# Attention over four query tiles in a two-block f32 transformer kernel: the order of the tiles, the steps of the modulation sums, and the form of GpSimd's scaling

## Chip, cores and metric

One core of a Trainium2 chip. The metric is the device time of one execution in microseconds (us). The engines are named as in the profile: PE (TensorE matmuls; PEld is its weight load), DVE (VectorE), ACT (ScalarE), POOL (GpSimd), SP (SyncE, which here only issues DMAs).

## What is computed

Two blocks over 512 tokens of width 1024, all in f32. The first block has two layers: half a SwiGLU FFN, a token mixer, half a SwiGLU FFN. The second block (adaptive norms, a retention and a gated linear attention mixer, two more FFNs) is not touched here, except that nine modulation vectors that it needs are summed early, inside the first block's attention. The mixer of a layer, cut to what matters:

```python
q_nope, q_rope, k, v = ...                    # MLA, 4 heads; keys of 96
s = jnp.where(kpos <= qpos, q @ k.T * scale, NEG)       # causal, in blocks of 128 queries
o_mla = softmax(s) @ v_mla
a = softmax(s[:, 0]) - lam * softmax(s[:, 1])           # differential, 4 heads x 2 maps
o_diff = rms_norm(a @ v_diff, g) * (1 - lam_init)
p_c = softmax(where(valid, q @ k_cmp.T, NEG)) * valid   # NSA, 8 heads: 31 compressed keys
o_nsa = g0 * (p_c @ v_cmp) + g1 * o_slc + g2 * o_win    # selected and window keys; gates
y = concat(o_mla, o_diff, o_nsa) @ w_out
m = silu(c) @ ada_w + ada_b                             # 9 x 1024, for the second block
```

With 512 tokens every selected and window map is a plain causal map, so all 28 maps of a query tile have the same keys: those of its own tile and of all earlier ones.

## The kernel before

Every engine runs its own hand-written instruction stream, and semaphores order them. A layer is: FFN, norm, projections, attention, output projection, FFN. The weights of all dense products go through four slots of SBUF (`w_raw`, split into `w_hi` and `w_lo` by ACT line 884 and POOL line 840), and dense products are three fp32r matmuls per 128x128 block (line 2060).

**Attention** runs once per layer (layer 0 from 584.5 us, layer 1 from 1762.4 us). Its work is cut into units of two maps: 14 units per query tile (`UN`; two of MLA, four of differential heads, eight of NSA, `UNIT_MAPS`), four tiles, so 56 units (`NU`). The tiles are taken in the order 0, 1, 2, 3. Tile i has (i+1)*128 keys, so the units grow from 128 to 512 columns. All five engines step through t = 0 to 60 in the same pipeline, i, step = divmod(t, 14):

- PE: scores of unit t with their causal mask (lines 2317, 2319) into one of two pairs of PSUM banks, which is free once the exponentials of two score groups earlier have been read; the transposes of the probabilities of unit t-3 (line 2347; the second map's wait for DVE's copy of the unit before); the outputs of unit t-4 (line 2390, accumulated in banks 6 and 7).
- DVE: the row maximum of unit t (line 1714), the copy of the second transposed map of unit t-3 (line 1723), the reciprocal of unit t-1's sums (line 1728).
- ACT: the copy of the first transposed map of unit t-3 (line 1126), the exponentials of unit t with their sums (line 1135).
- POOL: the scaling of unit t's probabilities by the reciprocals (lines 848 to 856), in place. NSA maps are scaled by two columns at once (the reciprocal and the gate, line 852), the second differential maps too (reciprocal and lambda, line 854); the MLA maps and the first differential maps by one (line 856, no second operand).

Once per tile there is more. At step 1 (`AT_CMP`) PE makes the compressed scores (line 2326), and DVE subtracts their maxima; at step 2 ACT takes their exponential (line 1141) and DVE sums, inverts and gates them (`cmp_sums`, lines 1679 to 1686); at step 6 they are transposed. At steps 10 to 13 the differential heads are normalized: ACT loads the table of the root and then that of the exponential again (two table loads), DVE inverts. At step 4 of the next tile (`AT_LAST`), or after the last step for the last tile, the outputs of the bank 7 are split into `h_hi` and `h_lo`. The output projection starts when the last of these is written.

**Adaptive sums.** The nine modulation vectors (`ada_w`, 9216 columns) are summed in 18 steps per layer. One such step is 16 matmuls of 128x32 by 256 columns (line 2409) at the end of PE's step t, DVE's copy of the result (line 1769, the last thing DVE does in step t), four tiny matmuls at PE's step t+1, right after its scores and ahead of its transposes (line 2334), and DVE's addition (line 1733). Which t have one is a table (line 89):

```python
ADA_STEPS = [UN * i + at for i, steps in enumerate(((6, 8), (1, 5, 7, 9), (1, 3, 5, 7, 9), (1, 3, 5, 7, 9), (1, 3))) for at in steps]
```

so two in tile 0, four in tile 1, five each in tiles 2 and 3, and two after the last scores (t = 57 and 59). Their weights come in halves through a ring of three (SP, line 757): three halves ahead of the attention, then four slots of `w_out` (line 663), and only then the fourth half and those behind it.

## Time and profile before

| | |
|---|---|
| time, median of 3 runs | 3871.97 us (3863.09 to 3878.66) |
| the profiled execution | 3891.44 us, of which its span 3889.7 us |
| PE busy | 3633.1 us, 93% of the span |
| DVE, ACT, POOL busy | 1371.2, 1289.6, 1441.1 us (35%, 33%, 37%) |
| mean clock granted to TensorE | 0.954 of full speed |
| attention, layer 0 and layer 1 | 584.5 to 801.3 us and 1762.4 to 1967.0 us: 216.8 and 204.6 us |
| DMA | 83 GB/s on average |

The profile is one execution, seen by the hardware profiler. Busy time of an engine counts its instructions, overlaps taken once; matmul ends are modelled. The granted clock is a share of full speed: at 1.0 TensorE runs at 2.4 GHz, at 0.5 at 1.2 GHz; numbers between are averages over a stretch.

### The profile page before, as it was taken

Reading aid. Unit: us, or ns where it says so; the run is one execution under the profiler, and the core shown is the slowest. Engines: PE = TensorE matmul, PEld = TensorE weight load, DVE = VectorE, ACT = ScalarE, POOL = GpSimd, SP = SyncE. Lnnn points to the kernel's source line nnn. Section 1 sums busy time; section 2 is a strip of 40 time slices with the busy share of each in tenths; the row PEclk is TensorE's granted clock in tenths of the full one; section 3 lists DMA queues with packets and bytes.
Section 4 is the critical chain, followed back from the end, with each engine's and each line's share of the span. In section 5 each row is a group of like instructions: output and inputs, shape, how many; then the busy total and the mean of one; then the engine's idle time right before and its main releaser. Section 6 shows DMA issues by size and latency. Waiting matters only on the chain. (4 is left out here: it accounts for less than half of the span.)

```text
span 3889.7 us, 50750 instructions
## 1 busy us (share of the span) xinstructions
PE 3633.1 (93%) x18374; PEld 2863.5 (74%) x18374; DVE 1371.2 (35%) x1921; ACT 1289.6 (33%) x2011; POOL 1441.1 (37%) x756
## 2 busy tenths in 40 slices
PE   7999899999999999798999996999998998779998
PEld 6888575578887888565578884888886785547886
DVE  4223544542325232554642326111114303552112
ACT  4223334543224222334543224312123234234222
POOL 4444233434444444334434442222222340013443
PEclk8999897999999999898999998999998998979999
DMA  4333342323333332342323332222212322012331
GB/s 133 95 96 91 75 122 77 108 69 96 95 91 98 95 96 87 73 127 87 110 68 96 96 91 72 59 65 60 65 53 56 86 82 65 1 44 81 97 97 60
DMA packets 569027, 322.35 MB, mean 83 GB/s; under 512 B 30266, under 2 KB 563360, under 8 KB 568480
## 3 DMA queue, kind: packets, MB, share of 16 engines
q1 hardware_dynamic: 568864, 320.22, 28.3%
q8 instruction: 97, 1.59, 0.2%
q14 instruction: 66, 0.54, 0.0%
HBM read 318.08 MB, written 2.10 MB: 82 GB/s over the span
## 5 line engine op out<-in xcount | busy, mean ns | idle before, releaser
L840 POOL TENSOR_TENSOR w_lo<-w_raw,w_hi 128x1024 fp32r<-128x1024 f32 x516 | 1267.7, 2457 | 2187.7 <-ACT w_hi L884 2187.7
L884 ACT ACTIVATE w_hi<-w_raw 128x1024 fp32r<-128x1024 f32 x516 | 547.6, 1062 | 1876.6 <-PE psum L2060 1767.6
L2060 PE MATMUL psum<-h_hi,w_hi 128*128 128x512 f32 x1328 | 544.1, 410 | 45.4 <-DVE h_ctx_lo L1457 22.8
L2060 PE MATMUL psum<-xg_hi,w_hi 128*128 128x512 f32 x1408 | 553.0, 393 | 12.2 <-DVE xg_lo L1409 10.4
L2060 PE MATMUL psum<-xg_lo,w_hi 128*128 128x512 f32 x1408 | 549.7, 390 | 0.0
L2060 PE MATMUL psum<-xg_hi,w_lo 128*128 128x512 f32 x1408 | 549.5, 390 | 0.0
L2060 PE MATMUL psum<-h_lo,w_hi 128*128 128x512 f32 x1328 | 530.3, 399 | 0.0
L2060 PE MATMUL psum<-h_hi,w_lo 128*128 128x512 f32 x1328 | 528.4, 398 | 0.0
L2060 PE MATMUL psum<-a_hi,w_hi 128*128 128x512 f32 x1232 | 433.3, 375 | 5.0 <-DVE a_lo L1525 4.2
L2060 PE MATMUL psum<-a_lo,w_hi 128*128 128x512 f32 x1232 | 434.2, 376 | 0.0
L2060 PE MATMUL psum<-a_hi,w_lo 128*128 128x512 f32 x1232 | 432.5, 374 | 0.0
L2060 PEld LDWEIGHTS psum<-h_hi,w_hi 128*128 128x128 f32 x1328 | 253.9, 191 | 133.1 <-issue 38.1
L2060 PEld LDWEIGHTS psum<-xg_hi,w_hi 128*128 128x128 f32 x1408 | 265.5, 189 | 72.2 <-DVE xg_lo L1409 14.0
L2060 PEld LDWEIGHTS psum<-xg_lo,w_hi 128*128 128x128 f32 x1408 | 265.6, 189 | 56.1 <-issue 1.2
L2060 PEld LDWEIGHTS psum<-xg_hi,w_lo 128*128 128x128 f32 x1408 | 265.5, 189 | 55.2
L2060 PEld LDWEIGHTS psum<-h_hi,w_lo 128*128 128x128 f32 x1328 | 254.4, 192 | 59.1
L2060 PEld LDWEIGHTS psum<-h_lo,w_hi 128*128 128x128 f32 x1328 | 254.9, 192 | 56.8 <-issue 5.4
L2060 PEld LDWEIGHTS psum<-a_hi,w_hi 128*128 128x128 f32 x1232 | 218.6, 188 | 49.9 <-DVE a_lo L1525 5.9
L2060 PEld LDWEIGHTS psum<-a_hi,w_lo 128*128 128x128 f32 x1232 | 219.6, 188 | 43.0
L2060 PEld LDWEIGHTS psum<-a_lo,w_hi 128*128 128x128 f32 x1232 | 219.1, 188 | 41.2
L1484 DVE TENSOR_TENSOR gated<-silu_g,psum 128x512 f32<-128x512 f32 x66 | 37.6, 597 | 501.3 <-ACT silu_g L937 501.3
L1520 DVE TENSOR_TENSOR gated<-psum,rstd 128x512 f32<-128x512 f32 x88 | 60.9, 692 | 420.8 <-PE psum L2060 420.8
(409 smaller groups left out, 4387.8 us busy)
## 6 DMA issues: line engine op xcount, KB each, us to landing
w_raw<-ffn_w SPq DMA_DIRECT2D x120, 512.0 KB, 3.8
w_raw<-ffn_w_gate SPq DMA_DIRECT2D x88, 512.0 KB, 3.8
w_raw<-ffn_w_up SPq DMA_DIRECT2D x88, 512.0 KB, 3.8
ada_raw<-ada_w SPq DMA_DIRECT2D x72, 512.0 KB, 4.5
w_raw<-ffn_w_down SPq DMA_DIRECT2D x64, 512.0 KB, 4.1
w_raw<-w_in SPq DMA_DIRECT2D x60, 512.0 KB, 3.8
w_raw<-ffn_w_down SPq DMA_DIRECT2D x32, 384.0 KB, 3.4
w_raw<-w_out SPq DMA_DIRECT2D x24, 512.0 KB, 4.0
```

What stands on the lines that cost most here:

```text
L840: nc.gpsimd.tensor_tensor(w_lo[:, i, :], w_raw[:, i, :], w_hi[:, i, :].bitcast(F32), ALU.subtract).then_inc(lo_ready, 1)
L884: nc.scalar.activation(w_hi[:, pos, :], w_raw[:, pos, :], ACT.Copy).then_inc(hi_ready, 1)
L1484: last = nc.vector.tensor_tensor(gated[:, i, o:o + n], silu_g[:, i, o:o + n], up, ALU.mult)
L1520: nc.vector.tensor_tensor(gated_1[:, i, :], psum[:, 3 * i + 1, :], rstd[:, 0:T], ALU.mult).then_inc(scaled.sem, 1)
L2060: last = nc.tensor.matmul(dst, w[:, pos, k * P:(k + 1) * P], rhs[g][r](k0 + k), start=k == 0 and m == 0, stop=k == nk - 1 and m == 2)
```

## The change

It does three things. The tiles are taken in the order 3, 2, 1, 0 (`TILE_AT`), so the units shrink from 512 to 128 columns; every use of the tile number that stands for tokens (queries, keys, gates, masks, places in `h_hi` and `h_lo`) goes through `TILE_AT`, while the counts of the semaphores go on by the order in time. The adaptive sums have the steps 0, 2, 5, 7, 9 of the first tile in time, 1, 3, 5, 7, 9 of the second and the third, 1, 5, 8 of the fourth, and none after the last scores. POOL's scaling of the MLA and first differential maps has a second column, `ones`. Outputs at a tile's first unit also wait for the adaptive sums in the first tile.

```diff
+TILE_AT = tuple(range(TT))[::-1]
-ADA_STEPS = [UN * i + at for i, steps in enumerate(((6, 8), (1, 5, 7, 9), (1, 3, 5, 7, 9), (1, 3, 5, 7, 9), (1, 3))) for at in steps]
+ADA_STEPS = [UN * i + at for i, steps in enumerate(((0, 2, 5, 7, 9), (1, 3, 5, 7, 9), (1, 3, 5, 7, 9), (1, 5, 8))) for at in steps]
...
             def attention(layer):
                 for u in range(NU):
-                    n = (u // UN + 1) * P
+                    tile = TILE_AT[u // UN]
+                    n = (tile + 1) * P
...
                         else:
-                            last = nc.gpsimd.tensor_scalar(rows, rows, inv, None, ALU.mult)
+                            last = nc.gpsimd.tensor_scalar(rows, rows, inv, ones[:, 0:1], ALU.mult, ALU.mult)
...
                         dve.wait_ge(*scores_done(layer, SCORE_AT["unit", t] + 1))
-                        nc.vector.tensor_reduce(neg_max[:, 2 * t:2 * t + 2], psum[:, b:b + 2, 0:(i + 1) * P], AX_X, ALU.max,
+                        nc.vector.tensor_reduce(neg_max[:, 2 * t:2 * t + 2], psum[:, b:b + 2, 0:(TILE_AT[i] + 1) * P], AX_X, ALU.max,
...
-                            for b in range(u // UN + 1):
+                            for b in range(TILE_AT[u // UN] + 1):
                                 last = nc.tensor.transpose(psum[:, 4 + m, b * P:(b + 1) * P], probs[:, u % 3, m, b * P:(b + 1) * P], ident[:])
...
-                        if at == 0 and j:
-
-                            pe.wait_ge(*diff_std(layer, 2 * j))
+                        if at == 0:
+                            if j:
+
+                                pe.wait_ge(*diff_std(layer, 2 * j))
                             pe.wait_ge(*ada_read(layer, 2 * sum(n <= t for n in ADA_STEPS)))
```

How the streams move, at the three places that the prediction speaks of. Rows of the change have its own line numbers, which are 1 to 5 higher.

PE at the start of the attention, before (steps 0 to 2; `ISA` and `REGISTER_ALU` are waits and counters):

```order
L2317 MATMUL psum<-k_mla,q_mla 128x128 x2
L2319 MATMUL psum<-causal_b,ident_b 128x128 x2
L2317 MATMUL psum<-k_mla,q_mla 128x128 x2
L2319 MATMUL psum<-causal_b,ident_b 128x128 x2
L2322 REGISTER_ALU
L2326 MATMUL psum<-k_cmp,q_nsa 128x31 x8
L2312 REGISTER_ALU
L2317 MATMUL psum<-k_diff,q_diff 128x128 x2
L2319 MATMUL psum<-causal_b,ident_b 128x128 x2
```

and now (steps 0 to 2, up to the first scores of step 2):

```order
L2321 MATMUL psum<-k_mla,q_mla 128x512 x2
L2323 MATMUL psum<-causal_b,ident_b 128x128 x2
L2412 REGISTER_ALU
L2414 MATMUL psum<-ada_raw,cond 32x256 x8
L2321 MATMUL psum<-k_mla,q_mla 128x512 x2
L2323 MATMUL psum<-causal_b,ident_b 128x128 x2
L2326 REGISTER_ALU
L2330 MATMUL psum<-k_cmp,q_nsa 128x31 x8
L2335 ISA
L2338 MATMUL psum<-cond_sum,mod_rows 128x2 x2
L2315 REGISTER_ALU
L2321 MATMUL psum<-k_diff,q_diff 128x512 x2
```

The left-out parts of the diff replace the tile's number by `TILE_AT` in the same way. The scores have 512 columns where they had 128, and an adaptive sum stands behind the first scores, its small matmuls behind the compressed scores, and another sum follows behind the scores of step 2.

DVE at steps 2 and 3 of the first tile, before:

```order
L1714 TENSOR_REDUCE neg_max<-psum 128x2
L1726 REGISTER_ALU
L1728 RECIPROCAL scaled_inv<-exp_sum 128x2
L1679 TENSOR_REDUCE cmp_stats<-cmp_p 128x8
L1680 REGISTER_ALU
L1681 RECIPROCAL cmp_stats<-cmp_stats 128x8
L1682 REGISTER_ALU
L1683 TENSOR_TENSOR cmp_stats<-cmp_stats,gates 128x8
L1685 REGISTER_ALU
L1686 TENSOR_SCALAR cmp_stats<-cmp_stats,cmp_any 128x8
L1713 REGISTER_ALU
L1714 TENSOR_REDUCE neg_max<-psum 128x2
```

and now:

```order
L1731 RECIPROCAL scaled_inv<-exp_sum 128x2
L1682 TENSOR_REDUCE cmp_stats<-cmp_p 128x8
L1683 REGISTER_ALU
L1684 RECIPROCAL cmp_stats<-cmp_stats 128x8
L1685 REGISTER_ALU
L1686 TENSOR_TENSOR cmp_stats<-cmp_stats,gates 128x8
L1688 REGISTER_ALU
L1689 TENSOR_SCALAR cmp_stats<-cmp_stats 128x8
L1769 REGISTER_ALU
L1772 COPY mod_rows<-psum 128x256
L1716 REGISTER_ALU
L1717 TENSOR_REDUCE neg_max<-psum 128x2
```

DVE's copy of the adaptive sum (`mod_rows`) of step 2 stands behind the whole of `cmp_sums`; before, no adaptive sum was at a step 2.

PE at the end of the attention, before:

```order
L2383 MATMUL psum<-cmp_pt,v_cmp 64x128 x2
L2390 MATMUL psum<-probs_t_134,v_slc 64x128 x8
L2390 MATMUL psum<-probs_t_132,v_win 64x128 x8
L2402 REGISTER_ALU
L2409 MATMUL psum<-ada_raw,cond 32x256 x8
L2331 REGISTER_ALU
L2334 MATMUL psum<-cond_sum,mod_rows 128x2 x2
L2414 REGISTER_ALU
L2415 REGISTER_ALU
L2418 ISA
L2060 MATMUL psum<-h_hi,w_hi 128x512
```

and now:

```order
L2351 MATMUL psum<-ident,probs 128x128 x2
L2395 MATMUL psum<-probs_t_132,v_win 64x128 x2
L2342 REGISTER_ALU
L2351 MATMUL psum<-ident,probs 128x128 x2
L2388 MATMUL psum<-cmp_pt,v_cmp 64x128 x2
L2395 MATMUL psum<-probs_t_134,v_slc 64x128 x2
L2395 MATMUL psum<-probs_t_132,v_win 64x128 x2
L2419 REGISTER_ALU
L2423 ISA
L2063 MATMUL psum<-h_hi,w_hi 128x512
```

The last transposes and outputs stand as x2 where they stood as x8 (one and four blocks of keys, for two maps or two heads), and the adaptive sum with its small matmuls is gone from between the last outputs and the output projection (line 2060, now 2063).

## Rows read from the trace of the kernel before

**Rows 1.** The page, share of the 40 slices: clock granted to TensorE, in tenths.
```profile
PEclk8999897999999999898999998999998998979999
```

**Rows 2.** Stretches: us, then PE, PEld, DVE, ACT, POOL busy (count), PEclk, DMA, GB/s.
```profile
584.50:624.40 39.90, 35.74 (x232) 21.66 (x232) 16.69 (x56) 18.54 (x76) 15.57 (x28) 0.60 0.21 69
624.40:673.30 48.90, 46.00 (x359) 28.18 (x356) 24.33 (x67) 23.22 (x78) 18.75 (x29) 0.77 0.27 87
673.30:729.80 56.50, 52.60 (x459) 32.36 (x458) 30.34 (x68) 27.65 (x78) 23.30 (x29) 0.88 0.30 94
729.80:786.00 56.20, 51.87 (x514) 33.22 (x512) 33.94 (x65) 30.09 (x72) 26.48 (x27) 1.00 0.31 95
786.00:801.30 15.30, 11.64 (x132) 9.03 (x132) 5.94 (x13) 4.03 (x9) 3.05 (x4) 0.89 0.11 36
1762.40:1800.50 38.10, 32.72 (x232) 19.89 (x232) 16.16 (x55) 18.28 (x76) 15.35 (x28) 0.69 0.22 72
1800.50:1842.60 42.10, 38.73 (x350) 23.84 (x348) 23.63 (x65) 23.17 (x80) 18.64 (x30) 0.91 0.33 101
1842.60:1893.80 51.20, 48.13 (x470) 30.64 (x466) 30.06 (x68) 28.04 (x80) 23.51 (x30) 0.97 0.33 104
1893.80:1949.40 55.60, 52.11 (x518) 33.27 (x514) 33.35 (x64) 30.22 (x73) 26.58 (x28) 1.00 0.31 96
1949.40:1967.00 17.60, 13.09 (x133) 10.20 (x133) 6.77 (x14) 4.03 (x9) 3.05 (x4) 0.81 0.11 31
```

**Rows 3.** The same columns, 10 us inside the first tile, layer 0.
```profile
600.00:610.00 10.00, 10.00 (x68) 5.98 (x60) 3.15 (x11) 2.33 (x12) 1.77 (x4) 0.50 0.52 167
```

**Rows 4.** Waits of PE in layer 0's attention: us in total, times, longest.
```profile
PE psum L2347 <- DVE probs_t L1723: 8.0, 5, 2.8
```

**Rows 5.** Groups by line on POOL: busy, mean ns, idle before.
```profile
L852 POOL TENSOR_SCALAR probs<-probs,scaled_inv,gates 128x128 f32<-128x128 f32 (+3 forms) x128 | 77.0, 612 | 156.4 <-DVE scaled_inv L1728 156.4
L856 POOL TENSOR_SCALAR probs<-probs,scaled_inv 128x128 f32<-128x128 f32 (+3 forms) x64 | 68.9, 1088 | 53.0 <-DVE scaled_inv L1728 53.0
```

**Rows 6.** Who waited for POOL's line 856: us, times.
```profile
  PEld psum L2347: 0.3, 1
```

**Rows 7.** Timeline of the first steps: start, us, engine, what [idle before].
```profile
586.70 1.08 PE L2326 MATMUL psum<-k_cmp,q_nsa 64*128 64x31 f32 x16 [0.74 <-ACT probs L1135]
...
590.44 0.80 PE L2317 MATMUL psum<-k_diff,q_diff 32*128 32x128 f32 x4 [1.02 <-ACT probs L1135]
```

**Rows 8.** Timeline of the 512-key tile, layer 0.
```profile
729.76 1.98 PE L2317 MATMUL psum<-k_mla,q_mla 96*128 96x512 f32 x4
...
740.24 0.40 ACT L1141 ACTIVATE cmp_p<-cmp_p 128x248 f32<-128x248 f32 x1
740.67 0.41 DVE L1679 TENSOR_REDUCE cmp_stats<-cmp_p 128x8 f32<-128x248 f32 x1 [1.22 <-ACT cmp_p L1141]
...
741.87 1.23 DVE L1714 TENSOR_REDUCE neg_max<-psum 128x2 f32<-128x1024 f32 x1
...
742.62 1.07 PE L2409 MATMUL psum<-ada_raw,cond 128*32 128x256 f32 x16
...
743.62 1.13 PE L2317 MATMUL psum<-k_diff,q_diff 32*128 32x512 f32 x4
...
743.76 0.42 DVE L1769 COPY mod_rows<-psum 128x256 f32<-128x256 f32 x1
...
744.38 0.20 ACT L1135 ACTIVATION_READ_ACCUMULATOR probs<-psum,neg_max 128x1 f32 x1
```

**Rows 9.** Timeline of SP's queue before and at layer 0's attention.
```profile
563.18 1.80 SPq L757 DMA_DIRECT2D ada_raw<-ada_w  x3
570.88 17.24 SPq L663 DMA_DIRECT2D w_raw<-w_out  x4
```

**Rows 10.** Timeline of the end of layer 0's attention.
```profile
785.52 1.23 DVE L1714 TENSOR_REDUCE neg_max<-psum 128x2 f32<-128x1024 f32 x1
...
801.33 0.49 PE L2060 MATMUL psum<-h_hi,w_hi 128*128 128x512 f32 x1 [1.19 <-DVE h_lo L1702]
```

More of the change, by code:

```diff
@@ L851, in attention @@
                             at = 3 * h + (1 if kind == "slc" else 2)
-                            last = nc.gpsimd.tensor_scalar(rows, rows, inv, gates[:, u // UN, at:at + 1], ALU.mult, ALU.mult)
+                            last = nc.gpsimd.tensor_scalar(rows, rows, inv, gates[:, tile, at:at + 1], ALU.mult, ALU.mult)
                         elif second:
@@ L1124, in attention @@
                             act.wait_ge(*o_done(layer, u - 1))
-                        n = (u // UN + 1) * P
+                        n = (TILE_AT[u // UN] + 1) * P
                         nc.scalar.activation(probs_t[u % 2][:, 0, 0:n], psum[:, 4, 0:n], ACT.Copy).then_inc(probs_t_act.sem, 1)
@@ L1129, in attention @@
                         act.wait_ge(*max_ready(layer, t + 1))
-                        n = (i + 1) * P
+                        tile = TILE_AT[i]
+                        n = (tile + 1) * P
                         for m in range(2):
@@ L1137, in attention @@
                         last.then_inc(exp_ready.sem, 1)
-                        at = slice(i * P, (i + 1) * P)
+                        at = slice(tile * P, (tile + 1) * P)
                         if step == AT_CMP_EXP:
@@ L1699, in last_low @@
                 def last_low(i):
-                    at = slice(i * P, (i + 1) * P)
+                    at = slice(TILE_AT[i] * P, (TILE_AT[i] + 1) * P)
                     dve.wait_ge(*o_hi_ready(layer, 3 * i + 3))
@@ L1721, in attention @@
                             dve.wait_ge(*o_done(layer, u - 1))
-                        n = (u // UN + 1) * P
+                        n = (TILE_AT[u // UN] + 1) * P
                         nc.vector.tensor_copy(probs_t[u % 2][:, 1, 0:n], psum[:, 5, 0:n]).then_inc(probs_t_dve.sem, 1)
@@ L1735, in attention @@
                     if t < NU:
-                        at = slice(i * P, (i + 1) * P)
+                        at = slice(TILE_AT[i] * P, (TILE_AT[i] + 1) * P)
                         if step == AT_CMP_TURN:
@@ L2312, in attention @@
                             pe.wait_ge(*scores_read(layer, v - 2))
-                        n = (i + 1) * P
+                        tile = TILE_AT[i]
+                        n = (tile + 1) * P
                         banks = [psum[:, score_banks(("unit", t)) + m, :] for m in range(2)]
@@ L2316, in attention @@
                             q, k, _ = key_values(*head)
-                            nc.tensor.matmul(banks[m][:, 0:n], q(slice(i * P, (i + 1) * P)), k(n), start=True, stop=False)
+                            nc.tensor.matmul(banks[m][:, 0:n], q(slice(tile * P, (tile + 1) * P)), k(n), start=True, stop=False)
                         for m in range(2):
@@ L2326, in attention @@
                                     last = nc.tensor.matmul(psum[:, score_banks(("cmp", i)) + g, c * CMP_BLOCK:c * CMP_BLOCK + NC],
-                                                            q_nsa[rows, c, i * P:(i + 1) * P], k_cmp[rows, :], start=True, stop=True)
+                                                            q_nsa[rows, c, tile * P:(tile + 1) * P], k_cmp[rows, :], start=True, stop=True)
                             last.then_inc(scores_done.sem, 1)
@@ L2383, in attention @@
                                 nc.tensor.matmul(o_place(kind, h), v_cmp[:, g, c * DV:(c + 1) * DV], cmp_pt[:, g, :], start=True, stop=False)
-                        for b in range(j + 1):
+                        for b in range(TILE_AT[j] + 1):
                             for x, head in enumerate(UNIT_MAPS[at]):
@@ L2390, in attention @@
                                 last = nc.tensor.matmul(o_place(kind, h), v(b), probs_t[u % 2][:, x, b * P:(b + 1) * P],
-                                                        start=first and b == 0, stop=final and b == j)
+                                                        start=first and b == 0, stop=final and b == TILE_AT[j])
                         last.then_inc(o_done.sem, 1)
```

8 lines of the change are left out of this document (4 added, 4 removed).

## The prediction

> **What bounds the kernel now.** I read the page first. PE is busy for 93% of the span, and no other engine for more than 37%, so a change in the attention counts only by what it does to PE: its work, its idle time, and its clock. The granted clock over the span [rows 1] is 7 tenths in the slice in which layer 0's attention begins (the seventh, from 583 us) and 8 in that of layer 1 (the nineteenth, from 1750 us).
>
> Next come the stretches of the two attentions [rows 2]: of layer 0 the four tiles in the order of time (128, 256, 384, 512 keys) and the end behind the last scores, then the same of layer 1. Three things can be taken from them.
> - Idle time of PE: length less busy time, 4.2 + 2.9 + 3.9 + 4.3 + 3.7 = 19.0 us in layer 0, 5.4 + 3.4 + 3.1 + 3.5 + 4.5 = 19.8 us in layer 1.
> - Time at half clock: the clock has two levels, 1.0 (2.4 GHz) and 0.5 (1.2 GHz), so a mean of 0.60 over 39.9 us is 2 x 0.40 x 39.9 = 31.9 us at 1.2 GHz. The five stretches give 31.9, 22.5, 13.6, 0 and 3.4, together 71.4 us in layer 0; and 23.6, 7.6, 3.1, 0 and 6.7, together 41.0 us in layer 1.
> - PE's work, if it all ran at 2.4 GHz: busy time less half of the time at 1.2 GHz, 197.9 - 35.7 = 162.2 us and 184.8 - 20.5 = 164.3 us. That the two layers agree to 2 us says that the split into work, idle time and clock holds: the 12 us by which layer 0's attention is longer are clock.
>
> So an attention is about 163 us of work, 19.4 us of idle time and 20 to 36 us that half clock costs. The 512-key tile had no half clock in either layer, the 128-key tile had it for most of its length. Ten microseconds inside that tile [rows 3] have PE busy for 10.00 of 10.00 us at a clock of 0.50: a PE that never rests is not enough to get 2.4 GHz back while its matmuls are those of the short tile (few columns, keys of 32 to 96 rows).
>
> What PE waits for in an attention is mostly one thing, DVE's copy of the second map at the ends of tiles: 8.0 us in 5 waits, the longest 2.8 us at the end of the last tile [rows 4]. There the two table loads on ACT and the inversion on DVE stand between a maximum and the copy behind it.
>
> **Part 1, POOL's second column.** The widths are the same mix in both groups [rows 5]: 612 ns with two columns, 1088 ns with one. 64 x (1088 - 612) is 30.5 us less on POOL, 15 per layer. PE waited for line 856 once, 0.3 us [rows 6], because the transposes come three steps later. Between 0.3 and 30.5 us I take the 0.3 us that is in a row: nothing. What hides it is the lag of three steps, some 12 us of PE's own work in a long tile against 3.1 us of POOL.
>
> **Part 2, the order of the tiles: work.** The same matmuls are issued, so 163 us stay. The pieces that move are the last three transposes and four outputs of 512 keys, which leave the end of the attention and go into the steps of the next tile.
>
> **Part 3, idle time at the start.** With 512 keys the pipeline fills more slowly. In us from the first scores, with the durations of [rows 7, 8]: scores 1.98 and mask 0.3, to 2.3; adaptive sum 1.1, to 3.4; second scores to 5.7. Compressed scores 1.1 and the four small matmuls 0.6 fill to 7.4, but the third scores wait for the second pair of exponentials, which ends 2.7 us after the maximum begins (741.87 to 744.58), at 8.4: 1.0 us idle. Third scores 1.3, adaptive sum 1.1, fourth scores 1.3, to 12.1. Now PE's next instruction is the small matmul of the adaptive sum of step 2, and it needs `mod_rows`, which DVE copies only behind `cmp_sums`. That chain starts at 9.7: maximum and exponentials 2.7, compressed exponential 0.4, `cmp_sums` 1.2 (740.67 to 741.87), copy 0.4, and about 0.5 for five handovers: 14.9. So 2.8 us more idle, and the first transposes are queued behind that wait. Together 3.8 us, where the timeline of before has gaps of 0.74 and 1.02 us [rows 7]: +2 us per layer. The sum at step 0 has its weights (issued by 565 us); the fourth half is issued only behind the fourth `w_out` slot, at 588.1 us [rows 9], and might cost up to 2 us, within the same wait.
>
> **Part 4, idle time at the end.** From the last maximum to the output projection it is 15.8 us now [rows 10], 11.6 of 15.3 us of it busy [rows 2]. With 128 keys the chain is short, some 6 us by the differences of the shapes, but the 9 to 10 us saved are mostly PE work that is done earlier instead. The idle part falls from 3.7 to about 3 us. The stall of 2.8 us ahead of it stays, since it is DVE's and ACT's, and has less PE work beside it. I take -1 us per layer for the end (between -3.7, all of it, and +2).
>
> Idle time in all: +1 us per layer, +2.
>
> **Part 5, the clock.** This is the term that decides. By place, time at 1.2 GHz per layer:
> - Start: the fill has more and longer idle gaps than the one that ended at half clock in both layers, so I expect the clock to fall there again, in spite of the sum at step 0. But it then meets 512-key steps, and the nearest rows of long tiles, 13.6 and 3.1 us in the 384-key tile, say that it comes back sooner than in the short one. I take 12 us; bounds 0 and 31.9.
> - The borders: 512 to 384 keys 0, as 384 to 512 now. 384 to 256: 4 us, between 0 and 13.6.
> - The 128-key tile, entered over a border that cost the clock in both layers when it was passed the other way: 32 us, from 23.6 (layer 1's first stretch) to 45 (31.9 plus 3.3 for one more sum at half clock and 10 for the steps that still turn 256 keys).
> - The end: 4 us, from 3.4 to 6.7. It can reach into the output projection.
>
> Together 52 us, at a cost of half, 26 us per layer and 52 for both, against 35.7 + 20.5 = 56.2 us now: -4 us. **Sum:** -4 + 2 + 0 = -2 us. The sum is made against the profiled execution (3891.4 us), which becomes 3889; the median of the runs is 19.5 us lower, and the same difference there gives 3870 us. The spread of the three runs alone is 15.6 us.
>
> The row says that a fully busy PE stayed at 1.2 GHz for 10 us and more. The Trainium skill (TensorE: Matmul & The Clock Gate, What's actually happening) has a rule that speaks otherwise: "activity releases the throttle". Taken as busy time it would have the short tile back at full clock soon after each gap; the trace does not bear this out, and by it the result would be that of rival A.
>
> **Rival A, the clock holds** (22%). The adaptive sums at steps 0 and 2 keep PE occupied through the fill, the long tiles run on at 2.4 GHz, and in the short tile the clock comes in high and stays for most of it. For it: the 512-key tiles had no half clock at all, though they have stalls of 1 us and more. Against it: [rows 3], and the 2.8 us wait of part 3. Time at half clock falls to some 15 us per layer, the cost from 56 to 15 us: -41 + 2 = -39, 3833 us. It counts as faster from 45 us less of half clock over both layers on.
>
> **Rival B, the clock falls at the start and stays** (14%). This is the one on the other side. The wait for `mod_rows` behind `cmp_sums` lets the clock fall when the most expensive steps begin, and it takes the whole of the first ten steps to come back, 40 us. Less 4 us idle this costs 18 us per layer where the forecast has 6: +24, 3894 us. It decides from about 33 us at half clock at the start of each layer. For it: 24 and 32 us in the first stretch now. Against it: those were short matmuls.
>
> **Rival C, POOL was on the path** (3%): up to 30 us faster, 3842 us. Only the 0.3 us speak for it.
>
> **Forecast: no change that can be measured** (61%), 3870 us. A measurement of this kernel can tell about 0.5%, 19 us, from no change. Faster: A and C, less the part of A that stays within 19 us, with some of the forecast's own tail, 0.24. Slower: B and a little of the forecast's tail, 0.14. Same 0.62. The forecast alone holds 3850 to 3891. To leave out no more than 2 in 10 the range goes down to 3836, near A, and up to 3894, to B.
>
> **What the profile would show.** POOL's group of line 856 at about 612 ns (and 30 us less in all), and no change from it. PE busy from the first scores with a gap of about 1 us ahead of the third and one of 2 to 3 us ahead of the first transposes, ended by DVE's `mod_rows`. From the last maximum to the output projection 6 us instead of 15.8. Half clock near the start for about 12 us, none in most of the 512- and 384-key tiles, and most of the 128-key tile at 0.5. I am wrong if the first tile shows 1.0 throughout and the last one over 0.8 (A), or if the first tile's mean clock is under 0.7 (B), or if PE's idle time per attention leaves 17 to 23 us.

## The result and the profile after

| | before | changed |
|---|---|---|
| median, five runs each, one session | 3868.17 us (3863.01 to 3878.66) | 3887.01 us (3886.33 to 3888.64) |
| ratio to before, 95% interval | | 1.0040 (1.0021 to 1.0059) |
| profiled execution, its span | 3891.44, 3889.7 us | 3887.43, 3885.7 us |

The changed kernel is slower by 0.40%, where the forecast was 3870 us and no change that can be measured. (The ratios are not quotients of the medians; the two medians here are 18.8 us apart, 0.49%.) One execution of before in the second session took 8161 us and is left out of the ratios. 0.40% is within the 0.5% that the prediction called the same, and 3887 us within its range of 3836 to 3894, but the interval lies wholly above 1. The two profiled executions say something else: there the changed kernel is 4 us shorter, and the forecast had 2 us. The experiments had to explain that contradiction first.

These are the ten stretches that answer to [rows 2], of the changed kernel. The tiles of each layer stand in the order of time, now 512, 384, 256 and 128 keys, then the end behind the last scores; columns as in [rows 2].

```profile
583.50:644.70 61.20, 58.29 (x467) 34.83 (x468) 30.95 (x58) 29.17 (x70) 21.11 (x26) 0.86 0.31 97
644.70:696.90 52.20, 48.28 (x498) 32.06 (x497) 30.56 (x67) 27.86 (x78) 19.46 (x29) 1.00 0.33 102
696.90:740.90 44.00, 40.34 (x413) 26.80 (x412) 24.63 (x67) 23.03 (x78) 16.23 (x29) 0.96 0.40 121
740.90:783.80 42.90, 39.02 (x278) 24.56 (x278) 19.26 (x63) 17.71 (x77) 12.71 (x28) 0.64 0.12 38
783.80:795.00 11.20, 6.05 (x41) 3.52 (x39) 4.82 (x11) 5.77 (x15) 2.29 (x6) 0.73 0.00 0
1757.80:1818.90 61.10, 58.19 (x466) 34.85 (x467) 30.89 (x58) 29.20 (x70) 21.11 (x26) 0.86 0.31 97
1818.90:1871.20 52.30, 48.38 (x498) 32.13 (x497) 30.64 (x67) 27.89 (x78) 19.47 (x29) 1.00 0.33 102
1871.20:1915.20 44.00, 40.35 (x413) 26.85 (x412) 24.60 (x67) 23.03 (x78) 16.23 (x29) 0.96 0.40 121
1915.20:1958.00 42.80, 38.92 (x278) 24.57 (x275) 19.26 (x63) 17.63 (x76) 12.66 (x28) 0.64 0.13 38
1958.00:1969.20 11.20, 6.05 (x42) 3.53 (x39) 4.82 (x11) 5.82 (x15) 2.33 (x6) 0.73 0.00 0
```

The two layers now take 211.5 and 211.4 us. The split of the prediction, for layer 0: busy 58.29 + 48.28 + 40.34 + 39.02 + 6.05 = 192.0 us, so 19.5 us idle. Half clock is twice (1 - mean clock) times the length: 17.1 + 0 + 3.5 + 30.9 + 6.0 = 57.5 us, 57.1 before rounding. Work is 192.0 - 28.6 = 163.4 us. Work and idle time are those of before; the clock is what differs.

Ten microseconds in the changed kernel's last tile, the row that answers to [rows 3]:

```profile
755.00:765.00 10.00, 10.00 (x65) 6.25 (x68) 4.44 (x17) 5.06 (x22) 3.90 (x9) 0.50 0.22 76
```

PE rests for not a moment and stays at half clock, as in the short tile before. The two scaling groups on POOL, against [rows 5] (by line; busy, mean ns):

```profile
L854 POOL TENSOR_SCALAR probs<-probs,scaled_inv,gates 128x512 f32<-128x512 f32 (+3 forms) x128 | 76.5, 607 | 144.6 <-DVE scaled_inv L1731 144.6
L858 POOL TENSOR_SCALAR probs<-probs,scaled_inv,ones 128x512 f32<-128x512 f32 (+3 forms) x64 | 38.7, 615 | 86.8 <-DVE scaled_inv L1731 86.8
```

The second column brings 1088 ns down to 615 ns, 30.2 us less on POOL, as forecast. Nobody gains by it in the waits: POOL itself sits idle for 86.8 us ahead of these 64 instructions, waiting for DVE, and no instruction is listed as waiting for them, where before had one wait of 0.3 us.

### The profile page after: what moved, and what is told of

Its sections match the earlier page's. It is cut to its first block and busy times, and to the rows that moved or that the text cites. A ratio compares the mean times of both kernels' runs of the same rounds, so it can differ in the third digit from the quotient of the medians.

```text
span 3885.7 us, 50748 instructions
## 1 busy us (share of the span) xinstructions
PE 3628.5 (93%) x18374; PEld 2863.3 (74%) x18374; DVE 1369.1 (35%) x1921; ACT 1288.0 (33%) x2011; POOL 1411.5 (36%) x756
## 5 line engine op out<-in xcount | busy, mean ns | idle before, releaser
L2063 PE MATMUL psum<-xg_hi,w_hi 128*128 128x512 f32 x1408 | 552.6, 392 | 12.0 <-DVE xg_lo L1412 10.3
```

What stands on the lines that cost most here:

```text
L2063: last = nc.tensor.matmul(dst, w[:, pos, k * P:(k + 1) * P], rhs[g][r](k0 + k), start=k == 0 and m == 0, stop=k == nk - 1 and m == 2)
```

## The experiments

### Session one: a second profile of before, and the three parts alone

`before_again` is the kernel before without an edit. `two_columns` is the kernel before with the one line

```diff
-    last = nc.gpsimd.tensor_scalar(rows, rows, inv, None, ALU.mult)
+    last = nc.gpsimd.tensor_scalar(rows, rows, inv, ones[:, 0:1], ALU.mult, ALU.mult)
```

`order_only` has `TILE_AT` reversed, with the old table of sums and one column; `sums_only` has the tiles in the old order, the new table and one column:

```diff
-ADA_STEPS = ... (((6, 8), (1, 5, 7, 9), (1, 3, 5, 7, 9), (1, 3, 5, 7, 9), (1, 3))) ...
+ADA_STEPS = ... (((0, 2, 5, 7, 9), (1, 3, 5, 7, 9), (1, 3, 5, 7, 9), (1, 5, 8))) ...
```

> The unchanged kernel once more, to get a second profile of it. The first one was 19.5 us longer than the median of its runs (3891.4 against 3872.0), and the prediction carried the difference over to the changed kernel unchanged. Theory 1, the place is the clock in the attentions: this profile's span is near 3866 us and shows some 40 us less half clock in the two attentions than the 112.7 us of the first (20 us at 2 us of half clock for 1 us of time), with work near 163 us and idle time near 19 us per attention. Theory 2, the place is elsewhere (dense stretches, start, DMA): the attentions are 216.8 and 204.6 us long again, and the 20 us are missing outside them. If the profile comes out at 3890 again, profiling itself adds the difference, and the changed kernel's profile (3887.4 us, equal to its runs) would speak against that.

> Part 1 alone: the kernel before with the second column of ones on POOL. Theory 1 (prediction): POOL's group of line 856 falls from 1088 to about 612 ns, 30 us less on POOL, and the time stays within 3 us of before, since PE waited 0.3 us for it. Rival (C of the prediction): POOL was on the path of the fill, up to 15 us faster per layer. A third way: with DVE and POOL moved against each other the clock's stretches shift, and the time moves by 5 to 15 us either way with no change in PE's idle time.

> Part 2 alone: the tiles from the longest to the shortest, with the table of adaptive sums and the one column of before. Theory 1, the order costs the time, because the short tile now runs whole at half clock (30.7 us of it in the changed kernel) and its units' stalls lie behind it: 3885 to 3895 us, the short tile at 0.5 as before, and two more adaptive sums behind the last scores, each about 2 us with its waits. Theory 2, the sums at steps 0 and 2 cost the time (the wait for mod_rows behind cmp_sums): without them 3 us of idle time per layer go, the first stretch of half clock is shorter than 17 us, and the time is 3870 us or less.

> The new table of the adaptive sums alone, with the tiles in the order of before (128 keys first). Theory 1: in the fill of the short tile five sums instead of two add about 5 us of dense work to a tile of 37 us; the clock falls in the fill all the same, since a PE that was fully busy stayed at half clock there, so the first stretch stays between 20 and 35 us, and the time is within 10 us of before. Rival: the sums from the first step hold the clock through the fill and the short tile; the first stretches (30.7 and 23.9 us in the first profile) go, and the time is 10 to 20 us shorter than before.

Twelve timed runs of each against 35 of before (median 3874.72 us). "Half clock" in this table and the later ones is us per attention at 1.2 GHz in the profiled execution, layer 0 / layer 1, summed as above but before rounding.

| | median us | ratio (95%) | attention us | half clock us |
|---|---|---|---|---|
| before_again | 3872.20 | 0.9998 (0.9979 to 1.0017) | 203.0 / 203.0 | 37.5 / 37.5 |
| two_columns | 3877.80 | 1.0014 (0.9998 to 1.0030) | 209.3 / 203.1 | 51.2 / 37.5 |
| order_only | 3873.20 | 0.9991 (0.9973 to 1.0009) | 201.5 / 212.1 | 30.7 / 54.6 |
| sums_only | 3874.37 | 1.0003 (0.9985 to 1.0022) | 204.7 / 198.4 | 37.5 / 23.9 |

The first row resolves the contradiction. The stretches of layer 0 in the second profile of the unchanged kernel (128, 256, 384, 512 keys, end; columns as above):

```profile
584.00:618.30 34.30, 31.40 (x221) 19.13 (x222) 13.31 (x50) 15.69 (x68) 14.60 (x26) 0.65 0.26 80
618.30:660.90 42.60, 38.62 (x350) 23.73 (x349) 24.09 (x66) 23.79 (x81) 18.44 (x29) 0.92 0.32 100
660.90:712.30 51.40, 47.59 (x454) 29.97 (x453) 30.42 (x69) 28.11 (x79) 22.99 (x29) 0.97 0.32 104
712.30:767.60 55.30, 51.21 (x507) 32.56 (x505) 33.48 (x66) 28.78 (x75) 27.24 (x29) 1.00 0.30 96
767.60:787.00 19.40, 14.35 (x164) 11.19 (x162) 8.61 (x15) 7.22 (x13) 3.48 (x5) 0.91 0.09 28
```

Half clock 24.0 + 6.8 + 3.1 + 0 + 3.5 = 37.4 us, busy 183.2, idle 19.8, work 164.5 us. In [rows 2] the same program had 71.4 us in this place, with work of 162.2 and idle time of 19.0 us: a difference of 34 us at half clock. The split prices that at 17 us of time; the attention's length shows 13.8 us (216.8 to 203.0), because work and idle time come out 2.3 and 0.8 us apart the other way. Against this profile the changed one is 17.3 us longer in its span (3885.7 - 3868.4), and its attentions are 16.9 us longer (422.9 - 406.0). So between these two profiles the slowdown lies wholly inside the attentions: half clock 75.0 to 114.3 us costs 19.7, work and idle time give back 2.8, together 16.9 us.

None of the three parts alone is measurably slower; together their ratios would make 1.0008. Each profile again splits into work of 164 to 166 us, 19 to 21 us idle, and half of the time at 1.2 GHz. What moves is where the clock falls, and two identical layers of one execution can differ (30.7 and 54.6 us in order_only).

The second profile is not the typical one either. Every timed run has its mean granted clock on record, and twice (1 - clock) times its length is its time at half clock, for the whole program. Over the 139 timed executions of before in the four sessions that is 328 us on average, with clocks from 0.952 to 0.961. The first profile has 355 us and the second 300, the one about as far above the mean as the other is below it. The time outside the attentions is not constant either: 3468.3 us in the first profile and 3462.4 in the second, and between 3452 and 3474 us in all 18 profiles.

### Session two: the sum at step 2, and filling the short tile

`after_again` is the changed kernel unedited. `sum_at_3` moves one sum by one step:

```diff
-... (((0, 2, 5, 7, 9), (1, 3, 5, 7, 9), (1, 3, 5, 7, 9), (1, 5, 8))) ...
+... (((0, 3, 5, 7, 9), (1, 3, 5, 7, 9), (1, 3, 5, 7, 9), (1, 5, 8))) ...
```

`before_fill` is the kernel before with six matmuls added ahead of the scores of each of the first 17 steps; they write to columns 384 to 511 of the score banks, which nothing reads there. `after_fill` has the same six in the changed kernel's last 14 steps (`if t >= NU - UN`).

```diff
+                        if t < UN + 3:
+                            for _ in range(3):
+                                for m in range(2):
+                                    nc.tensor.matmul(banks[m][:, 3 * P:4 * P], ident_b[:], causal_b[:], start=True, stop=True)
```

> The changed kernel once more, beside the runs of before on the same chip. Split of the attention so far (work at full clock, idle time, half clock, all per attention): the kernel before in its second profile 164.4, 19.9, 37.5 us, the changed one 163.4, 19.5, 57.1 us, so all of the 8.4 us per attention by which it is longer is clock. Theory 1: the short tile at the end always runs at half clock; the profile again has 30.7 us there and some 57 us per attention, and the median is 10 to 20 us above before. Rival: how the stretches of half clock fall differs from session to session (before had 71.7 and 41.0 us in one profile, 37.5 and 37.5 us in another); then this profile has another number, the runs spread over 20 us as those of before do, and the difference to before is under 10 us.

> The changed kernel with the first tile's second adaptive sum at step 3 instead of step 2, so that its small matmuls no longer wait for mod_rows behind cmp_sums. Theory 1 (part 3 of the prediction): PE's idle time per attention falls by 2 to 3 us and the gap ahead of the first transposes by as much; and if that gap is what brings the clock down at the start, the first stretch of 17 us is gone or is 10 us as in the kernel with the order alone: 4 to 10 us faster per layer. Rival: the first fall comes from the fill as such; the stretch stays at 17 us, and only the idle time goes, 2 us per layer.

> The kernel before with six more matmuls per step (128x128 by 128 columns, bf16, the identity by the mask, into PSUM columns that nothing reads) ahead of the scores, in the 14 steps of the 128-key tile and the first three of the next. They compute nothing that is used. Each takes some 0.055 us at full clock, so 17 steps cost 5.6 us of PE work per attention. Theory 1, what keeps the short tile at half clock is how little its matmuls give the array to do (a PE busy for 10.00 of 10.00 us stayed at 0.50): the 23.9 us stretch in the first tile goes or is under 10 us, and the attention is 3 to 8 us shorter than 203 us in spite of the work. Rival, the clock follows the gaps in the fill alone: the first stretch stays near 24 us, the added matmuls cost double there, and the attention is 6 to 10 us longer.

> The changed kernel with the same six matmuls per step in the 14 steps of its last tile, the one with 128 keys, 4.6 us of work per attention. Theory 1: the 30.7 us at half clock in that tile go for the most part, the tile falls from 42.9 to some 32 us, and the kernel gains 10 to 20 us over both layers, to about the time of before or below it. Rival: the fall comes at the border from 256 to 128 keys and holds whatever follows: the tile stays at half clock and is 8 us longer per layer.

| | median us | ratio (95%) | attention us | half clock us |
|---|---|---|---|---|
| after_again | 3880.49 | 1.0019 (1.0002 to 1.0036) | 211.4 / 202.4 | 57.2 / 33.5 |
| sum_at_3 | 3868.14 | 0.9977 (0.9958 to 0.9996) | 201.7 / 198.8 | 30.5 / 23.4 |
| before_fill | 3858.08 | 0.9953 (0.9935 to 0.9971) | 195.8 / 195.8 | 3.4 / 3.4 |
| after_fill | 3873.32 | 1.0000 (0.9985 to 1.0015) | 204.6 / 202.4 | 30.1 / 23.4 |

**The changed kernel again.** 12 runs go from 3867.34 to 3891.33 us, where the first five lay within 2.3 us. Layer 1 had no fall in its last tile (3.4 us instead of 30.7), and its attention is 9.0 us shorter. All intervals for this kernel lie above 1, here and in session three, but nearer to 0.2% than to the 0.40% of the first five runs, and in both later sessions the lower end is 1.0002. The plain medians are 3.3 and 6.3 us above before (0.09% and 0.16%).

**The sum at step 2.** These two kernels were timed side by side and their intervals do not overlap. What PE did in the changed kernel from its second mask on (timeline: start, us, what, idle before):

```profile
588.29 0.28 PE L2323 MATMUL psum<-causal_b,ident_b 128*128 128x128 bf16 x2
588.49 1.08 PE L2330 MATMUL psum<-k_cmp,q_nsa 64*128 64x31 f32 x16
589.50 0.61 PE L2338 MATMUL psum<-cond_sum,mod_rows 128*128 128x2 f32 x4
591.36 2.08 PE L2321 MATMUL psum<-k_diff,q_diff 32*128 32x512 f32 x4 [1.25 <-ACT probs L1138]
593.37 0.39 PE L2323 MATMUL psum<-causal_b,ident_b 128*128 128x128 bf16 x2
593.69 1.94 PE L2414 MATMUL psum<-ada_raw,cond 128*32 128x256 f32 x16
595.56 2.08 PE L2321 MATMUL psum<-k_diff,q_diff 32*128 32x512 f32 x4
597.57 0.39 PE L2323 MATMUL psum<-causal_b,ident_b 128*128 128x128 bf16 x2
598.37 1.01 PE L2338 MATMUL psum<-cond_sum,mod_rows 128*128 128x2 f32 x4 [0.41 <-DVE mod_rows L1772]
599.24 1.95 PE L2351 MATMUL psum<-ident,probs 128*128 128x128 f32 x8
```

and in sum_at_3:

```profile
589.05 0.61 PE L2338 MATMUL psum<-cond_sum,mod_rows 128*128 128x2 f32 x4
590.91 2.08 PE L2321 MATMUL psum<-k_diff,q_diff 32*128 32x512 f32 x4 [1.25 <-ACT probs L1138]
592.92 0.39 PE L2323 MATMUL psum<-causal_b,ident_b 128*128 128x128 bf16 x2
593.24 2.08 PE L2321 MATMUL psum<-k_diff,q_diff 32*128 32x512 f32 x4
595.25 0.39 PE L2323 MATMUL psum<-causal_b,ident_b 128*128 128x128 bf16 x2
595.43 1.90 PE L2351 MATMUL psum<-ident,probs 128*128 128x128 f32 x8
597.27 1.07 PE L2414 MATMUL psum<-ada_raw,cond 128*32 128x256 f32 x16
598.27 1.13 PE L2321 MATMUL psum<-k_diff,q_diff 32*128 32x512 f32 x4
```

Both stop for the same 1.25 us ahead of the third scores, and both are at half clock behind it: scores of this shape take 2.08 us. In sum_at_3 the clock is back at 597.3 us (a sum in 1.07 us, scores in 1.13); in the changed kernel a sum takes 1.94 us, and full speed comes only at about 608. The first tile thus has 6.8 us of half clock instead of 17.1, in both layers. So the clock falls at the stall for the third scores in both, and the sum at step 2 puts off the return by 10 us. The edit moves the sum together with its small matmuls, so it does not show whether the 16 matmuls or the wait for `mod_rows` do this. That wait is only 0.41 us long here: at half clock PE is busy while DVE catches up.

The first tile is the smaller part of what this edit gains, though. In layer 0 of the two profiles, half clock falls from 57.1 to 30.5 us: 10.3 us less in the first tile, 6.8 more in the 256-key tile, and 23.9 less in the last tile, whose steps the edit does not touch. That tile in the two layers of sum_at_3, where the changed kernel has a clock of 0.64 twice (columns as in [rows 2]):

```profile
739.50:773.50 34.00, 29.13 (x278) 18.96 (x275) 18.86 (x63) 17.41 (x76) 12.63 (x28) 0.90 0.15 48
1898.80:1933.80 35.00, 30.24 (x279) 19.57 (x277) 18.84 (x63) 17.47 (x76) 12.71 (x28) 0.85 0.15 47
```

How one sum in the first tile changes the clock of the last, 150 us later, no run shows.

I had expected less idle time from this edit. It has more, 21.0 and 21.6 us against 19.5. The gain is clock only; that a faster PE reaches the same waits earlier is my reading, not tested.

**The fill.** In before_fill the short tile holds full clock throughout. Its first three stretches of layer 0:

```profile
584.10:614.30 30.20, 27.72 (x308) 19.01 (x306) 13.58 (x51) 16.30 (x70) 14.69 (x26) 1.00 0.30 89
614.30:654.40 40.10, 36.22 (x361) 22.81 (x360) 23.41 (x66) 23.08 (x79) 18.54 (x29) 1.00 0.34 106
654.40:705.10 50.70, 46.06 (x453) 29.03 (x452) 30.39 (x69) 28.19 (x79) 23.09 (x29) 1.00 0.33 105
```

The added matmuls of the first tile (groups by line and form: busy, mean ns, idle before):

```profile
L2318 PE MATMUL psum<-causal_b,ident_b 128*128 128x128 bf16 x89 | 7.5, 220 | 0.4 <-ACT probs L1135 0.4
```

Against before_again the attention has 34.1 us less at half clock, which is worth 17.0 us, for 9.5 us of added work (173.9 against 164.4) and 0.3 us more idle: 7.2 us, which is what its length shows (203.0 to 195.8). I had put the added work at 5.6 us; it cost 9.5. The whole profiled execution is 24.1 us shorter than that of before_again, of which the two attentions have 14.4; the other 9.7 us lie where the edit does nothing, so one profile against one other overstates it. The timed runs say 0.47%, 18 us. PE was busy for less of the time at the higher clock; over the same 10 us:

```profile
600.00:610.00 10.00, 9.38 (x108) 6.01 (x105) 4.21 (x17) 5.30 (x25) 4.42 (x10) 1.00 0.57 180
```

In after_fill the last tile holds the clock in both layers (3.4 us at half clock in each). In layer 0 that is worth 13.6 us, of which the added work takes 7.3 (170.7 against 163.4 us); the first tile's 17.1 and 13.7 us stay.

### Session three: how little filling is enough

`fill_thin` is before_fill with matmuls that load and drive 32 columns of the array instead of 128 (`banks[m][0:32, ...]`, `ident_b[:, 0:32]`). `fill_two` has two of the matmuls a step, `range(1)` for `range(3)`. `sums_fill` is sums_only with its first sums at 0, 3, 5, 7, 9 and two matmuls a step. `after_third` is the changed kernel again.

> The kernel before with six more matmuls per step in the same 17 steps as in the run before_fill, with the same 128 columns each and so nearly the same time on PE, but with 32 columns of the array in use instead of 128 (output on 32 partitions). They compute nothing that is used. In before_fill the half clock of an attention fell from 37.5 to 3.4 us and the attention from 203.0 to 195.8 us. Theory 1, it is how much of the array works that holds the clock: with a quarter of it the short tile falls to half clock again, 15 us or more per attention, and the attention is 202 us or longer. Theory 2, it is that PE has something to do at all (the gaps filled): the half clock stays at 3 to 10 us and the attention near 195 us.

> As before_fill, with two more matmuls per step instead of six, 17 steps (nothing that is used is computed). The six cost 9.5 us of work per attention (173.9 against 164.4 us). If two hold the clock as well, the attention is near 195.8 - 6 = 190 us, and the kernel some 10 us faster than before_fill. If two are too few, 10 to 24 us of half clock come back in the first tile, and it is between before_fill and before.

> The tiles in the order of before (128 keys first), the new table of sums with the first tile's second sum at step 3 instead of 2 (0, 3, 5, 7, 9), no sums behind the last scores, two more matmuls per step in the first 17 steps (nothing that is used is computed), one column on POOL. If dense work in the short tile holds the clock, the five sums and the two matmuls do it together: half clock under 10 us per attention, the end 15.7 instead of 19.4 us as with the sums alone, attention 190 us or less. If not, it has 24 to 37 us of half clock as with the sums alone (198.4 and 204.7 us).

> The changed kernel a third time, to settle how far it is from before: so far 1.0040 (1.0021 to 1.0059) and 1.0019 (1.0002 to 1.0036). Its profiles had the last tile at 42.8 us with 30.7 us of half clock three times and at 32.4 us with 3.4 us once. If the last tile takes the one or the other by chance, the runs spread over 20 us again (3867 to 3891 us last time) and the ratio is between 1.000 and 1.005. If the first session was the rule, they lie together near 3887 us.

| | median us | ratio (95%) | attention us | half clock us |
|---|---|---|---|---|
| fill_thin | 3866.29 | 0.9970 (0.9954 to 0.9985) | 199.2 / 199.1 | 13.7 / 13.7 |
| fill_two | 3868.40 | 0.9973 (0.9953 to 0.9993) | 199.5 / 199.4 | 23.9 / 23.9 |
| sums_fill | 3869.47 | 0.9978 (0.9959 to 0.9997) | 204.5 / 204.6 | 37.5 / 37.5 |
| after_third | 3881.99 | 1.0020 (1.0002 to 1.0038) | 211.4 / 205.2 | 57.2 / 39.8 |

The two short tiles of fill_thin, layer 0:

```profile
584.60:614.70 30.10, 28.05 (x306) 19.26 (x306) 13.72 (x51) 16.32 (x70) 14.60 (x26) 1.00 0.29 89
614.70:654.50 39.80, 36.22 (x361) 22.82 (x360) 23.22 (x66) 22.90 (x79) 18.45 (x29) 1.00 0.36 107
```

A quarter of the array's columns was enough for the short tile: its clock was 1.00 with 32 columns as with 128. This went against the theory that the share of the array decides. Yet the 384-key tile, which has no added matmul in either kernel, had 10.2 us at half clock where before_fill had none. Two matmuls a step still halve the fall in the short tile (13.7 us against 23.9). sums_fill was a miss: more sums and a filler in the short tile, and 20.5 us at half clock in it all the same, where sums_only had 10.2. That I cannot explain from these rows. Nor does its profile explain its ratio: the attentions are 3 us longer than those of before_again (409.1 against 406.0 us), while the timed runs are 0.22% faster than before, with an interval below 1.

### Session four: the column once more, the sum at step 3 once more, and combinations

`after_one_col` is the changed kernel with POOL's old form for the 64 maps. `sum_at_3_b` is sum_at_3 unedited. `sum3_fill` adds the thin matmuls of fill_thin in its last 14 steps. `fill_no_tail` is before_fill with no sums after the last scores:

```diff
-... (((6, 8), (1, 5, 7, 9), (1, 3, 5, 7, 9), (1, 3, 5, 7, 9), (1, 3))) ...
+... (((4, 6, 8), (1, 3, 5, 7, 9), (1, 3, 5, 7, 9), (1, 3, 5, 7, 9))) ...
```

> The changed kernel with POOL's scaling as before, one column (line 856 at 1088 ns). Theory 1, the column is worth nothing in the new order too: the ratio is 1.002 to 1.004, as the changed kernel's. Rival 1, with 512 keys first POOL's 3.1 us per unit come onto the path of the fill: 1 to 3 us slower per layer than the changed kernel. Rival 2, the column shifts the stretches of half clock and costs: the kernel with the order alone and one column was at 0.9991, so this one is at 0.999 too.

> The kernel with the first tile's second sum at step 3 once more, on another day's chip beside the changed kernel with one column. Last time it was 0.9977 (0.9959 to 0.9996) of before where the changed kernel was 1.0019. If the place of that one sum is what makes the changed kernel slower than before, the ratio is below 1.000 again and the first stretch of half clock is 7 us (17 and 14 us in the changed kernel). If it was the luck of one session, the ratio is near 1.002.

> The changed kernel with the sum at step 3 and, in the last tile, six added matmuls of 32 columns of the array per step (nothing that is used is computed). If both places of half clock are closed in this way, an attention has 7 us of it at the start, 0 to 10 at the borders and 6 at the end: 195 to 199 us, ratio 0.996 or below. If the added work (some 7 us per attention by the run after_fill) eats what the clock gives back, it is at 0.998, as the sum at step 3 alone.

> The best kernel so far (before_fill: the order of before, six added matmuls per step in the first 17 steps, 195.8 us per attention, ratio 0.9953) with the two sums behind the last scores moved to step 4 of the first tile and step 3 of the second. In the runs with the sums alone the end fell from 19.4 to 15.7 us. If the moved sums cost their 1.7 us each where they go and their waits behind the last scores (1.1 + 1.8 us) go, the attention is 193 us, 5 us less over both layers: 0.994. Rival: the added steps bring half clock back, and it is at 0.996 or above.

| | median us | ratio (95%) | attention us | half clock us |
|---|---|---|---|---|
| after_one_col | 3880.26 | 0.9996 (0.9980 to 1.0012) | 204.6 / 204.5 | 36.4 / 36.4 |
| sum_at_3_b | 3867.73 | 0.9969 (0.9950 to 0.9987) | 201.8 / 198.8 | 30.4 / 23.4 |
| sum3_fill | 3871.81 | 0.9981 (0.9964 to 0.9999) | 199.5 / 208.2 | 16.4 / 36.8 |
| fill_no_tail | 3859.02 | 0.9942 (0.9921 to 0.9962) | 196.0 / 194.6 | 6.8 / 3.4 |

Before, timed beside these four, has a median of 3881.05 us. sum_at_3_b repeats its result. Filling the last tile as well adds nothing to it (the intervals overlap); in layer 1 of that profile the first tile had 20.5 us at half clock in spite of the sum at step 3, so that the cure of the first tile is not a sure one (6.8 us in five of the six attentions with it). fill_no_tail has the shortest end of all the old orders, 14.5 us for 19.4, and beats both kernels by the best ratio of the study, though not measurably more than before_fill alone. The end of layer 0, after the last scores:

```profile
765.90:780.40 14.50, 10.18 (x125) 8.21 (x123) 7.53 (x11) 7.21 (x13) 3.47 (x5) 1.00 0.00 1
```

The column stays open. The changed kernel was at 1.0019 and 1.0020 with two columns and at 0.9996 with one; before was at 1.0014 with two. Both pairs point to a loss of 0.15 to 0.25% by the faster POOL, in neither do the intervals part, and the pairs were not all timed in one session. No wait in the profiles would carry it, only the clock. And after_one_col, which has the sum at step 2 and no filling, had 10.2 us at half clock in its last tile in both layers, and 20.5 us in its first.

## Why the prediction was wrong, point by point

**The failed step is the last one of the sum**: "the median of the runs is 19.5 us lower, and the same difference there gives 3870 us". The sum itself, made against the profiled execution, said 3891.4 - 2 = 3889 us, and the changed kernel's profiled execution was 3887.4 us. But the 19.5 us were not an offset that any kernel has. They came for the most part from the term that the change replaces, which was mis-sized: "35.7 + 20.5 = 56.2 us now" is the cost of 112.4 us at half clock in the two attentions of one profile, and the second profile of the same program has 75.0, a cost of 37.5. With 75.0 in place of 112.4, the forecast's own 104 us of half clock is a loss of 14.5 us, and with +2 for idle time it makes 16.5 us slower.

How much slower the typical execution should be depends on the typical value, and the timed runs put that between the two: 328 us for the whole program, where the profiles have 355 and 300. As an estimate, half way between the profiles' attentions is 94 us, a cost of 47, and the forecast's 52 + 2 against it gives 7 us slower. Measured were 19 us by the medians of the first session, and in the later ones 7 to 8 by the ratios (0.19% and 0.20% of 3877) or 3 and 6 by the medians. The first session had luck of its own: the changed kernel's five runs have a mean clock of 0.9548, some 351 us at half clock, and the twelve of each later session 0.9576 and 0.9558, some 329 and 343 us.

What gave it away in the rows was there: the two layers of [rows 2] run the same program and had 71.4 and 41.0 us. I read the difference as proof that the split holds, and not as a sign that one of them was exceptional. The profiled execution also lay outside the range of the three runs (3891 against 3863 to 3879 us). None of the three signs by which I would have called myself wrong came (first tile 0.86, last 0.64, idle time 19.5 us): all of them looked at the changed kernel, and the error was in the number for the kernel before.

**Part 1, POOL's column: nothing.** The 30 us went from POOL, as said, and the attention's waits show none of them. Whether 0.2% comes in through the clock is open.

**Part 2, work stays 163 us: right** (163.4 and 163.3).

**Part 3, idle time at the start: half right.** The gap ahead of the third scores is 1.25 us (forecast 1.0). The one for `mod_rows` is 0.41 us (forecast 2.8), because the clock had already fallen and PE's own work covered DVE's chain. I had worked out the waits at full clock, and the clock apart from them; they are not independent. In all, idle time did not move: 39.0 us in the two attentions, before 38.8, where the forecast had 2 more.

**Part 4, the end: right in size.** From the last maximum to the output projection it is 7.0 us (787.95 to 794.96; forecast 6, before 15.8):

```profile
787.95 0.42 DVE L1717 TENSOR_REDUCE neg_max<-psum 128x2 f32<-128x256 f32 x1
...
794.96 0.79 PE L2063 MATMUL psum<-h_hi,w_hi 128*128 128x512 f32 x1 [1.51 <-DVE h_lo L1705]
```

The stall ahead of it stayed, but is 2.3 us. The waits of PE behind the last scores of layer 0 (us, times, longest) have what took the place of the adaptive sums there:

```profile
PE psum L2351 <- DVE probs_t L1726: 2.3, 1, 2.3
PE psum L2063 <- DVE h_lo L1705: 1.5, 1, 1.5
PE psum L2351 <- ACT probs_t L1128: 1.4, 1, 1.4
```

From the last scores' mask on, PE is idle for 11.2 - 6.05 = 5.2 us, and in the second profile of before for 19.4 - 14.35 = 5.1 us: no change where -1 was forecast. And the first matmul of the projection runs at half clock (0.79 us, where [rows 10] has 0.49).

**Part 5, the clock: right place by place.** Forecast 12, 4, 32 and 4 us for the start, the borders, the 128-key tile and the end. The profile has 17.1, 3.4, 30.7 and 6.0, and 4.3 more in the output projection's first matmuls. Together 57 where the forecast had 52. That the last tile fits is partly luck of the draw: in layer 1 of the two later profiles it has 3.4 and 10.2 us, and the 384- to 256-key border 10.2.

**The rivals.** A (the clock holds) did not come. The rule of the Trainium skill that I set against the row (TensorE: Matmul & The Clock Gate, What's actually happening) is that activity releases the throttle. Taken as busy time, it fails in the changed kernel as it did before: the row from 755 to 765 us has PE busy for 10.00 of 10.00 us at 0.50. In before_fill the added matmuls hold the clock at 1.00 with PE busy for 9.38 of 10 us, which busy time alone does not explain either. C did not come. B has a right place and the wrong amount: the first tile is at half clock for 17 us and not 40, the clock falls at another stall, and 6.8 of the 17 us stay when the sum is moved.

**The cause, as far as shown.** In the profiles the changed kernel's attentions lose by half clock alone, at two places: behind the start, and in the short tile at the end, which fell for 30.7 us in four of six profiled attentions and for 3.4 and 10.2 us in the others. Moving one sum by one step takes the kernel from 1.0019 to 0.9977, and repeated 0.9969, so the place of that sum does decide; but both places have less half clock with it, and the runs do not say what each is worth. Filling the last tile alone gives 1.0000 and the old column on POOL 0.9996, both with intervals that overlap the changed kernel's. So the loss of some 0.2% is not pinned to one part of the change. Why the short tile falls in one execution and not in the next is not shown.

## What to carry to other kernels

Before an edit is costed, take a second profile of the unchanged kernel, or compare stretches in it that run the same program: a term that differs between them (here 71.4 and 41.0 us at half clock) is one that has to be costed from its typical value, not from the execution in hand. Two profiles can miss on either side; the mean clock of the timed runs says where they lie. Split a stretch into work, idle time and half clock, and remember that the last two mix: a wait worked out at full clock can vanish behind a slower PE and come back with a faster one. In the first steps of a pipeline, try the place of a sum whose small matmuls depend on another engine's long chain: here one step later made the kernel 0.4% faster, a gain that the waits alone would not have shown.

## What had not been expected

- Unused work makes the kernel faster: six matmuls of 128 columns in each of 17 steps, 9.5 us of work per layer, take 7.2 us off each attention of the profile (ratio 0.9953).
- The same number of matmuls that use 32 of the array's 128 columns holds the clock in the short tile too (1.00 over 30.1 us).
- Matmuls of 512 columns are no guarantee: behind a stall of 1.25 us the first tile ran for 6.8 us at half clock at best.
- One program's attention takes 203.0 or 216.8 us, with work within 3 us and idle time within 1 us of each other.
- Moving one sum in the first tile left the last tile, 150 us later, at 6.8 and 10.2 us of half clock where the changed kernel mostly had 30.7.
